# An S5 prologue: the input load no longer waits for the small loads, TensorE runs twenty products ahead of the sum of squares, and the modulation units are dealt out sooner

## What is computed

```python
cond = jax.nn.silu(c)
mod = cond @ ada_w[i] + ada_b[i]                 # 1024 x 6144 weights
sh_t, sc_t, g_t, sh_c, sc_c, g_c = jnp.split(mod, 6, axis=-1)
h = modulate(rms_norm(x, norm_g[i, 0]), sh_t, sc_t)
h = s5_mixer(h, a_re, a_im, log_dt, b_re, b_im, c_re, c_im, d_skip, w_glu)
```

## Time and profile before

| | |
|---|---|
| time, median of 3 runs | 1266.87 us (1266.48 to 1266.88) |
| the profiled execution's own time | 1267.49 us |
| its span, first to last instruction | 1265.7 us |
| share of the span in which TensorE is busy | 96% |
| start of the first product of the gated unit (L1882) | 137.29 us |

### The profile page before, as it was taken

One profiled execution on the slowest core, in us unless ns is written; L12 is line 12 of the kernel. 1 busy time (PEld: TensorE's weight loads), 2 busy tenths in 40 slices (PEclk: granted clock), 3 DMA queues, 4 the chain that ended last, 5 costly groups with the idle time before them and its releaser, 6 DMA issues.

```text
span 1265.7 us, 17622 instructions
## 1 busy us (share of the span) xinstructions
PE 1214.5 (96%) x6439; PEld 973.7 (77%) x6439; DVE 765.5 (60%) x1077; ACT 527.1 (42%) x809; POOL 384.7 (30%) x261
## 2 busy tenths in 40 slices
PE   4987999999999999999999999999999999999997
PEld 2756888778888887888788777678788888887886
DVE  8989577868976345242783687867744444442225
ACT  3282454243444334131432577756444434441211
POOL 4971100245644344000122534510343343331000
PEclk9998999899999999999899999999999999999999
DMA  7858555244752222223124232211032222223221
GB/s 282 360 185 224 201 199 200 100 166 170 293 201 100 100 100 100 100 100 115 64 76 141 67 97 87 67 67 67 34 130 85 88 95 99 99 99 120 86 94 67
DMA packets 26696, 162.19 MB, mean 128 GB/s; under 512 B 4496, under 2 KB 4816, under 8 KB 8400
## 3 DMA queue, kind: packets, MB, share of 16 engines
q1 hardware_dynamic: 25632, 161.15, 36.3%
q10 hardware_dynamic: 1008, 0.28, 0.1%
HBM read 152.76 MB, written 2.10 MB: 122 GB/s over the span
## 4 chain that ended last, share of the span: by engine, by line
PE 84%; DVE 7%; DMA 3%; issue 3%; ACT 2%; SPq 1%; ACTq 0%; DVEq 0%; POOL 0%
PE psum L1882 17%; PE psum L1884 17%; PE psum L1883 17%; PE psum L1996 3%; PE psum L2089 3%; PE psum L1998 3%; PE psum L2091 3%; PE psum L2090 3%; PE psum L1997 3%; PE psum L1759 2%; DMA ada_raw<-in_ada_w 2%; PE psum L2146 1%; PE psum L1724 1%; PE psum L2167 1%; PE psum L2132 1%
## 5 line engine op out<-in xcount | busy, mean ns | idle before, releaser
L1882 PE MATMUL psum<-hhi,whi 128*128 128x512 f32 x960 | 377.9, 394 | 3.9 <-DVE wlo L1279 3.4
L1884 PE MATMUL psum<-hhi,wlo 128*128 128x512 f32 x960 | 374.0, 390 | 0.0
L1883 PE MATMUL psum<-hlo,whi 128*128 128x512 f32 x960 | 373.8, 389 | 0.0
L1279 DVE TENSOR_TENSOR wlo<-raw,whi 128x2048 fp32r<-128x2048 f32 x81 | 194.6, 2402 | 176.2 <-ACT whi L715 176.2
L715 ACT ACTIVATE whi<-raw 128x2048 fp32r<-128x2048 f32 x80 | 153.1, 1914 | 165.6 <-PE psum L2091 76.4
L1882 PEld LDWEIGHTS psum<-hhi,whi 128*128 128x128 f32 x960 | 180.6, 188 | 46.2 <-DVE wlo L1279 4.8
L559 POOL TENSOR_TENSOR ca<-ca,cb 128x512 f32<-128x512 f32 x44 | 142.0, 3227 | 238.0 <-ACT ca L840 238.0
L1884 PEld LDWEIGHTS psum<-hhi,wlo 128*128 128x128 f32 x960 | 180.2, 188 | 38.2
L1883 PEld LDWEIGHTS psum<-hlo,whi 128*128 128x128 f32 x960 | 180.4, 188 | 36.0
L1444 DVE SCALAR_TENSOR_TENSOR ca<-psum,convp,ca 128x511 f32<-128x511 f32 x44 | 33.0, 749 | 208.0 <-ACT ca L836 208.0
L842 ACT ACTIVATE ghi<-ca 128x512 f32 (+1 forms) x44 | 27.8, 632 | 154.8 <-POOL ca L559 154.8
(11 more groups left out here) (366 smaller groups left out, 1846.7 us busy)
## 6 DMA issues: line engine op xcount, KB each, us to landing
raw<-in_units SPq DMA_DIRECT2D x92, 1024.0 KB, 4.8
ada_raw<-in_ada_w SPq DMA_DIRECT2D x24, 1024.0 KB, 7.8
ada_ring<-in_ada_w SPq DMA_DIRECT2D x24, 1024.0 KB, 4.8
qk_sw<-ca SPq DMA_DIRECT2D x32, 128.0 KB, 2.3
u<-in_x_blocks SPq DMA_DIRECT2D x1, 2048.0 KB, 7.6
x<-in_x_t SPq DMA_DIRECT2D x1, 2048.0 KB, 8.1
out_rows<-y_late SPq DMA_DIRECT2D x8, 256.0 KB, 2.1
bc_par<-in_s_bc SPq DMA_DIRECT2D x1, 1024.0 KB, 5.4
```

The source lines that it names most:

```text
L1279: TT(wlo[:, s, :], raw[:, s, :], whi[:, s, :].bitcast(F32), ALU.subtract).then_inc(split_lo, 1)
L1882: M(out, w_hi, hi[:, k, :], start=(k == 0), stop=False)
L1883: M(out, w_hi, lo[:, k, :], start=False, stop=False)
L1884: return M(out, w_lo, hi[:, k, :], start=False, stop=(k == KT - 1))
```

## The change

SyncE issues `u` and behind it the modulation units without the wait for the small loads. `cond` gets a semaphore of its own, `cond_in`, for which Silu waits; the other six small loads keep `small_in`, now 6 times 16, and ScalarE waits for it ahead of the wait for `u` and the squares. TensorE runs 20 products of `ones` with `ident` into PSUM bank 7, which nothing reads, once `ident`, `ones` and `cond` are ready and ahead of its first sum of squares. Of the modulation units five instead of three stand ahead of the first half of `turned_inputs(0)`, one instead of two between its halves, and units 13 and 14 stand ahead of `inputs(0)` instead of behind it.

```diff
@@ SyncE
-            sp.wait_ge(small_in, 16 * 7)
             sp.dma_start(u[:], a["x_blocks"].rearrange("p (g b) -> p g b", g=GROUPS)).then_inc(u_in, 16)
             for n in range(21):
                 load_ada0(n)
@@ GpSimd
             decay_tile(1)
-            pool.wait_ge(small_in, 16 * 7)
+            pool.wait_ge(small_in, 16 * 6)
@@ ScalarE
-                act.dma_start(dst, a[name]).then_inc(small_in, 16)
+                act.dma_start(dst, a[name]).then_inc(small_in if i else cond_in, 16)
             act.wait_ge(par_in, 16)
             A(s5s[:, 3, :], s5s[:, 2, :], ACT.Tanh, scale=1.0 / 16).then_inc(tanh_ready, 1)
-            act.wait_ge(small_in, 16 * 7)
+            act.wait_ge(cond_in, 16)
             A(cond[:, 1, :], cond[:, 0, :], ACT.Silu).then_inc(cond_ready, 1)
...
+            act.wait_ge(small_in, 16 * 6)
             act.wait_ge(u_in, 16)
             uf = u[:, :, :].rearrange("p g b -> p (g b)")
             for q in range(8):
@@ TensorE
             pe.wait_ge(sel_ready, 1)
+            pe.wait_ge(ident_ready, 1)
+            pe.wait_ge(const_ready, 1)
+            pe.wait_ge(cond_ready, 1)
+            for _ in range(20):
+                M(psum[:, 7, 0:P], ones[:], ident[:], start=True, stop=True)
             for q in range(8):
                 pe.wait_ge(usq_ready, q + 1)
                 M(psum[:, 7, :], blk16[:].rearrange("p g c -> p (g c)"), sq[:, q % 2, :], start=(q == 0),
                   stop=(q == 7)).then_inc(usq_summed, 1)
-            pe.wait_ge(cond_ready, 1)
             pe.wait_ge(row_clear, 1)
...
             pe.wait_ge(lb_zero, 4)
-            ada_units(0, 3)
+            ada_units(0, 5)
             turned_inputs(0, (0, 1))
-            ada_units(3, 5)
+            ada_units(5, 6)
             turned_inputs(0, (2, 3))
-            ada_units(5, KT)
+            ada_units(6, KT)
             turned_inputs(1)
...
+            ada_units(13, 15)
             pe.wait_ge(cl_dve, 1)
             inputs(0)
-            ada_units(13, 16)
+            ada_units(15, 16)
```

More of the change, by code:

```diff
@@ L219, in build @@
         sel_ready = sem("sel_ready")
+        cond_in = sem("cond_in")
         ident_ready, const_ready, cond_ready = (sem("ident_ready"), sem("const_ready"),
```

## The result

| | before | changed |
|---|---|---|
| median of the runs | 1266.88 us (1266.48 to 1267.52, 4 runs) | 1279.74 us (1279.32 to 1281.47, 4 runs) |
| the profiled execution's own time | 1267.49 us | 1279.92 us |
| first gated product starts | 137.2 us | 145.0 us |
| from there to the end of the span | 1128.5 us | 1133.1 us |

The ratio is 1.0098, with a 95% interval from 1.0084 to 1.0112. The direction holds, and so does the step that the forecast rested on, the small load that comes late. The forecast of 1272.2 us (1265 to 1276) is too low by 7.5 us, and the time lies outside the range, because of steps behind that one.

What follows compares the result with a forecast made beforehand. Bound: the chain of waits, mostly TensorE, to the K block's end at 84.93 us. First turned_inputs 11.2 us later, less 5.9 given back, is 5.3; 1266.87 + 5.3 = 1272.2 us, range 1265 to 1276.

Steps and rivals of the forecast that it cites:

- the small load that comes late: Ahead of ScalarE's squares: the last small load lands at 22.5 us, so the first square starts 7.3 us later.
- What the input load gains, and the turns: DMA queues: u lands at 11.6 us, 3.6 sooner; small packets alternate one for one with large, landing last at 22.5.
- The first rival: Small loads go in larger turns or first, landing before u; K block ends 5.5 us sooner, 1261.4 us; chance 0.12.
- the second: Rival: ScalarE's queue gets about two packets a turn; small loads land at 15.5, time 1265 to 1267 us; chance 0.07.
- The products cost nothing: TensorE's 20 unused products end between 12 and 17 us, before the squares at 22.5: no cost, and their gain lost.
- the sum: Shift of the K block's end: first turned_inputs 11.2 us later, less 5.9 given back, makes 5.3 us later.
- Unit 4: Ahead of the first turned_inputs: issued at 34.3, lands 4.7 us later at 39.1; turned_inputs starts at 40.0 instead of 28.77.
- What is given back until the K block: From the first turned_inputs to the K block's end: 1.8 + 1.06 - 0.3 + 2.35 + 0.95 = 5.9 us saved.
- What comes behind it starts later as a block: Everything behind the K block's end moves with it unchanged: 5.3 us later, first gated product at 142.6 us.

Runs made afterwards that it cites:

- E5: Changed kernel without the 20 products: 1276.13 us, ratio 1.0069 to the kernel before.
- E9: E4 without the 20 products: 1263.22 us, ratio 0.9962 to the kernel before.
- E14: E4 with 64 products one column wide instead of its 20 products: ratio 0.9987 to the kernel before.
- E16: E4 with its 20 products made one column wide: ratio 1.0013 to the kernel before.
- E2: Kernel before with only the loads and waits changed, no products, old unit order: 1275.89 us, ratio 1.0065.
- E6: Changed kernel with the modulation units in the order of before: 1276.35 us, ratio 1.0066 to the kernel before.
- E1: Changed kernel with SyncE's wait for the small loads put back ahead of the input load: 1267.81 us, ratio 1.0000.
- E3: Changed kernel with ScalarE's wait for the six small loads moved behind the eight squares: ratio 1.0008 to the kernel before.
- E4: Changed kernel with SyncE's wait for the six small loads put between the input load and the first modulation unit: ratio 0.9991.

## Why the prediction was wrong, step by step

**What the input load gains, and the turns.** Right, nearly to the digit. `u` landed at 11.75 (11.6 forecast), the last small load at 22.94 (22.5), the first square started at 22.96, and the sums ended at 33.07 (33.4). The first rival, larger turns, would have needed `rope_c` by 9.7, and the second, two small packets a turn, is excluded by 506 against 500. The rule of the Trainium skill that a DMA engine drains a packet of 9 to 17 descriptors from one queue before it turns to the next ("DMA: Bandwidth & Descriptors", Queues, rings and completion order) holds here in the going round and not in the size: a turn was one row.

**"The products cost nothing."** This step failed: the sum put them at nothing. The reasoning looked only at TensorE's time: they end long before anything needs the engine, which is so, and their warming is lost, which is so too. What costs is their 80 records in TensorE's program, which move all later work against the blocks of 256: some 0.3% of the time, or 3 to 4 us, by E5 and E9 and, on one chip, by E14 to E16.

**Unit 4.** The mechanism is right and the size was off. It was issued at 34.09 (34.3 forecast), but landed after 6.84 us instead of 4.7, and the `turned_inputs` behind the wait took 4.91 us instead of 3.77, at the low clock. Together 2.1 and 1.1 us more. The sum took the wait itself, and not that TensorE's work behind its 4.37 idle us would run at the low clock, as the row from 41.42 to 44.83 us shows.

**What is given back until the K block.** The pieces came nearly as put down: no wait for unit 7, units 13 and 14 in the wait for the modulated `u`, of which 0.8 us is left, `inputs(0)` in 2.0 us. But the K block took 9.2 us instead of 6.8, with 4.8 us of standing still against 2.6, which the sum had as a constant. 11.5 us at its end instead of 5.3: 2.1 + 1.1 from unit 4, 2.4 here, 0.6 left over, about what unit 4's own products took too long (1.51 us instead of 0.9).

**"What comes behind it starts later as a block."** This failed twice. Behind the K block 3.7 us came back, mostly for a reason that I should have read in the trace of before: its Toeplitz products ran partly at the low clock, and in the changed kernel they didn't; they also waited less for their tile. The two rows are of the kernel before and of the changed one, over the first 150 us:

```profile
L1813 PE MATMUL psum<-toep,u 128*64 128x128 f32 x128 | 11.2, 349 | 6.7 <-DMA toep<-kx 6.7
```

```profile
L1818 PE MATMUL psum<-toep,u 128*64 128x128 f32 x128 | 7.9, 276 | 4.0 <-DMA toep<-kx 4.0
```

And behind the first gated product 4.6 us were lost (1133.1 against 1128.5), where nothing was edited: in longer low stretches of the clock, 3.1 of it at the third barrier.

So by the books of the profiled executions: 7.8 us of the 12.4 lie ahead of the first gated product, where 5.3 were forecast, and 4.6 behind it, where none was. By the ratios: the loads' turns with ScalarE's wait cost 0.65% alone (E2), the new unit order on top of it nothing or little when there are no products (E5 against E2), the products nothing without the new order (E6 against E2), and both together 0.3% more. That the two parts cost only together is what the ratios say, over several chips and with differences hardly above what groups differ by; it isn't explained.

**What stays open.** By which path 80 records make the later parts slower; how the loss of 12.9 us divides between the products, unit 4 and the order, to better than 0.2%; why unit 4 took 2 us longer than its like in most other profiles (there is one profile of it); and why E1, E3 and E4 gain 2 to 4 us up to the first gated product in their profiles and at most 1 in their ratios.

## What to carry to other kernels

Ahead of small loads on one queue, a deep backlog of large ones on another is a trap: each small row pays for a large one. Count the rows on both sides; if the small loads are needed soon, hold back the large ones that are not, as E4 does with one line, or put the wait for the small ones where they are used. Idle-time filler on an engine is not free either: instructions take room in the program, and a stretch of many short ones can run out of instructions at the end of a block. And a gain that the profile shows at one point should be followed to the end of the span, and over many runs, before it is believed.

## What the runs showed of the hardware beyond what was expected

- Two DMA queues with work on the same engines took turns row by row: 506 small rows against 500 of 8 KB; the small ones had 7.5% of the engines' time.
- TensorE stood still for 0.3 to 3.4 us at fixed places of its program 256 records apart, when it ran short matmuls there (8 ns a record), and went on 1.2 to 1.5 us behind the landing of a packet of 16,384 bytes on the queue `q8 instruction`, in 32 stretches of 32. 80 records more moved the place by 40 matmuls, and 256 didn't move it.
- 1 MB issued into an idle DMA landed after 4.6 to 6.8 us.
- Work ran at the granted clock of 0.50, 1.2 GHz, at the end of and behind the waits of 9.8 and 4.4 us in the changed kernel, and the sum of such stretches differed from run to run of one kernel; in the runs of E1 it went with a time from 1265.0 to 1271.8 us.
